# A two-layer hybrid backbone on one core: order of the modulation, of the products in the RWKV doubling and of its scan, layers written out

## What is computed

```
mod = silu(cvec) @ w_ada + b_ada            # shift, scale, gate: 6 x 512 columns, two condition vectors
h = rmsnorm(x) * (1 + scale) + shift
z = h @ w_in                                # 74 tiles of 128 columns
y_a = hyena(z)                              # filters from a small MLP with two sines, long convolution by FFT
y_b = rwkv7(z)                              # two directions, 8 heads of 64
y_c = diff_attention(z)
x = x + gate * ((g_a*(y_a@w0) + g_b*(y_b@w1) + g_c*(y_c@w2)) @ w_out)
```

```
sa = S @ (-kk_t);  S = S * w_t + outer(sa, kk_t * a_t) + outer(v_t, k_t);  y_t = S @ r_t
```

## Time and profile before

| | |
|---|---|
| time, median of 3 runs | 3057.24 us (3052.05 to 3060.49) |
| the profiled execution | 3055.59 us, its span 3053.9 us |
| TensorE busy | 2821.3 us, 92% |
| VectorE, ScalarE, GpSimd busy | 1167.8, 628.5, 161.1 us |
| mean granted clock of TensorE | 0.93 |

### The profile page before, as it was taken

One profiled execution on the slowest core, in us unless ns is written; L12 is line 12 of the kernel. 1 busy time (PEld: TensorE's weight loads), 2 busy tenths in 40 slices (PEclk: granted clock), 3 DMA queues, 4 the chain that ended last, 5 costly groups with the idle time before them and its releaser, 6 DMA issues.

```text
span 3053.9 us, 57422 instructions
## 1 busy us (share of the span) xinstructions
PE 2821.3 (92%) x25584; PEld 1753.7 (57%) x25584; DVE 1167.8 (38%) x1890; ACT 628.5 (21%) x1182; POOL 161.1 (5%) x192
## 2 busy tenths in 40 slices
PE   7999998988898889999999999988889899899998
PEld 2546664575757575555525557545757576655554
DVE  4252725745454631100142536356353636311111
ACT  2111124322232321000031111243232323200000
POOL 0010000010101000000000100000101010000000
PEclk9999999979787989999999999998797888899999
DMA  6211110100000001111161111101000000011111
GB/s 241 95 45 55 49 56 7 43 5 29 5 29 4 30 3 56 62 62 62 56 213 56 45 55 57 41 14 36 4 30 3 30 10 23 14 59 62 62 55 62
DMA packets 38273, 147.13 MB, mean 48 GB/s; under 512 B 4720, under 2 KB 4720, under 8 KB 37136
## 3 DMA queue, kind: packets, MB, share of 16 engines
q1 hardware_dynamic: 34704, 128.47, 12.6%
q0 software_dynamic: 3328, 15.02, 1.3%
HBM read 139.27 MB, written 4.19 MB: 47 GB/s over the span
## 4 chain that ended last, share of the span: by engine, by line
PE 84%; DVE 8%; issue 3%; ACT 3%; DMA 1%; POOL 0%; DVEq 0%; POOLq 0%; another core or an unknown queue 0%; ACTq 0%
PE ps L508 82%; DVE scr L1687 1%; DVE scr L1709 1%; DVE scr L1866 1%; DVE scr L1700 1%; DVE scr L1822 1%; PE ps L873 1%; DVE scr L1859 1%; PE ps L966 1%; DVE scr L1699 0%; ACT scr L1397 0%; PE ps L764 0%; DVE scr L1862 0%; ACT scr L1398 0%; DVE scr L1833 0%
## 5 line engine op out<-in xcount | busy, mean ns | idle before, releaser
L508 PE MATMUL ps<-h,ring 128*128 128x512 f32 (+1 forms) x4480 | 1230.5, 435 | 3.2 <-issue 3.2
L508 PEld LDWEIGHTS ps<-h,ring 128*128 128x128 f32 x4480 | 685.3, 191 | 548.6 <-issue 547.6
L508 PE MATMUL ps<-scr 32*32 32x32 f32 (+9 forms) x17704 | 821.0, 246 | 122.4 <-issue 48.6
L508 PEld LDWEIGHTS ps<-scr 32*32 32x32 f32 (+5 forms) x17704 | 625.4, 140 | 306.1 <-issue 203.0
L1915 DVE SCALAR_TENSOR_TENSOR scr<-scr,ps 128x640 f32<-128x640 f32 x48 | 39.4, 821 | 509.3 <-PE ps L508 508.8
L1455 ACT ACTIVATE scr<-ps 128x640 f32<-128x640 f32 x48 | 33.8, 704 | 561.3 <-PE ps L508 561.3
L508 PE MATMUL ps<-scr,ring 128*128 128x512 f32 (+1 forms) x512 | 139.0, 434 | 4.0 <-DVEq L1920 4.0
L1411 ACT ACTIVATE scr<-ps 128x160 f32<-128x160 f32 x192 | 62.5, 325 | 279.0 <-PE ps L508 278.2
L508 PEld LDWEIGHTS ps<-scr,ring 128*128 128x128 f32 x512 | 77.4, 191 | 65.6 <-issue 65.6
L508 PE MATMUL ps<-scr,cst 128*128 128x512 f32 (+1 forms) x288 | 92.7, 459 | 9.6 <-ACT scr L1375 9.6
L508 PE MATMUL ps<-ring,sc 128*2 128x512 f32 x192 | 88.5, 616 | 8.3 <-ACT lora L1142 8.3
(11 more groups left out here) (254 smaller groups left out, 2189.2 us busy)
## 6 DMA issues: line engine op xcount, KB each, us to landing
ring<-in_w SPq DMA_DIRECT2D x240, 512.0 KB, 3.3
x<-in_x SPq DMA_DIRECT2D x1, 2560.0 KB, 15.8
yc<-in_win POOLq DMA_DIRECT2D x2, 1280.0 KB, 7.8
out_y<-x POOLq DMA_DIRECT2D x1, 2560.0 KB, 7.7
scr<-in_inv POOLq DMA_DIRECT2D x2, 1152.0 KB, 5.3
scr<-in_tab POOLq DMA_DIRECT2D x4, 512.0 KB, 8.9
cst<-in_cst POOLq DMA_DIRECT2D x1, 1466.0 KB, 9.3
scr<-in_ck POOLq DMA_DIRECT2D x2, 256.0 KB, 3.3
```

Source lines behind the costliest of these rows:

```text
L508: return nc.tensor.matmul(out, lhsT, rhs, start=start, stop=stop)
```

## The change

- The modulation leaves the front. A row is now made by four matmuls a slot, each with a stationary side of 128x32 and 256 columns, that write four different quarters of the partitions; small products with a constant matrix `pick` add up the quarters and turn the row. Layer 0's shift and scale come before everything (16 slots, with the squares of x between them), layer 1's between the tiles of layer 0's `w_out`, with the squares of x, and each layer's gate between the gate tiles of attention.
- h is taken tile by tile by the first tile of z. The filter MLP and the filters stand between the first tiles of z, and on VectorE the windows between the taps.
- In the RWKV doubling, A's blocks come ahead of the transposes of K and B. Products go by pairs of chunks into banks 4 and 5 and are read before the next pair: B by ScalarE (1024 columns, 1024, 512), K by VectorE with its mask, within levels 2, 3 and 4. The turned A goes to bank 4 and is copied for itself, the values' products to bank 5.
- In the scan, R comes in by a matmul with the identity in front of `reader`'s product (all four latent chunks), and VectorE's two additions fall away. Transitions and readers are copied together. The values' parts of y move behind the first state step, the state terms of K behind U.
- y is stored in eight pieces by SyncE, each when its tile of x is done.
- The loops over the layers are written out; the last layer makes no modulation. The number of slots stays 240.

```diff
-ORDER = [("filt",)] + [("ada", n, q) for n in range(6) for q in range(4)]
+ADA = [("ada", n, q) for n in range(4) for q in range(4)]
...
-ORDER += [("z", f"av{j}") for j in range(JT)] + [("z", f"ag{j}") for j in range(JT)]
+ORDER += [("z", f"av{j}") for j in range(JT)]
+for _j in range(JT):
+    ORDER += [("z", f"ag{_j}")] + GATE[2 * _j:2 * _j + 2]
...
-ORDER += [("out", j) for j in range(KD)]
+for _j in range(KD):
+    ORDER += [("out", _j)] + ADA[2 * _j:2 * _j + 2]
...
+            for k in range(KD):
+                sp.wait_ge(out_read, k + 1)
+                sp.dma_start(A["y"][:, k * T:(k + 1) * T], xt(k)).then_inc(y_stored, 16)
+            sp.wait_ge(y_stored, 16 * KD)
...
+            def rows_of_mod(bank, q, w):
+                for kk in range(2):
+                    k = 2 * q + kk
+                    for half in range(2):
+                        at = 64 * kk + 32 * half
+                        o = kk * 512 + half * 256
+                        i = mm(ps[at:at + 32, 512 * bank:512 * bank + 256], sc[:, 32 * k:32 * k + 32], w[:, o:o + 256], q == 0, q == 3)
+                i.then_inc(w_used, 1)
+            def turn_row(cols, row):
+                for c in range(4):
+                    half = c // 2
+                    i = mm(cols[:, 2 * c:2 * c + 2], row[:, c % 2 * 128:(c % 2 + 1) * 128], con("pick")[:, 2 * half:2 * half + 2], True, True)
+                return i
...
+            for n in range(4):
+                if n >= 1:
+                    pe.wait_ge(pre_row, n)
+                for q in range(4):
+                    i = 4 * n + q
+                    pe.wait_ge(w_full[i % RING], 16 * (i // RING + 1))
+                    rows_of_mod(0, q, ringslot(i))
+                    if n in (1, 2):
+                        k = 4 * n - 4 + q
+                        pe.wait_ge(pre_sq, k + 1)
+                        sum_of_squares(k).then_inc(pre_sq_used if k < KD - 1 else sums_ready, 1)
+                if n >= 1:
+                    turn_row(mod_bank[:, 8 * (n - 1):8 * n], modrow[(n - 1) % 2]).then_inc(pre_turned, 1)
+            pe.wait_ge(pre_row, 4)
...
+                z_tile("hv0", as_h_comes=True, first_marks=True)
+                z_tile("hx0")
+                pe.wait_ge(hid_ready, 1)
+                wide_mm(6, fw[64:128, 0:64], hid[64:128, :], rows=slice(0, 64)).then_inc(hid_full, 1)
+                z_tile("hv1")
+                pe.wait_ge(hid_ready, 2)
+                filters(0)
+                filters(1)
+                z_tile("hx1")
+                filters(2)
+                filters(3)
+                z_tile("hv2")
+                filters(4)
+                z_tile("hx2")
+                turn_p(0)
+                z_tile("hv3")
+                turn_p(1)
+                z_tile("hx3")
...
+                        def products_of_B(c):
+                            pe.wait_ge(A_read, 4 * g + c // 2)
+                            product(Bt, c, 0)
+                            product(Bt, c + 1, 1).then_inc(A_full, 1)
+                        def products_of_context():
+                            pe.wait_ge(A_read, 4 * g + 2)
+                            product(Bt, 4, 0)
+                            product(Kt, 4, 1).then_inc(A_full, 1)
+                        def products_of_K(c):
+                            pe.wait_ge(A_read, 4 * g + 3)
+                            pe.wait_ge(K_read, 3 * g + 1 + c // 2)
+                            product(Kt, c, 0)
+                            product(Kt, c + 1, 1).then_inc(A_full, 1)
+                        def read_side():
+                            pe.wait_ge(K_read, 3 * g + 3)
+                            for c in range(4):
+                                i = nc.tensor.transpose(ps[:, 2048 + c * 128:2048 + (c + 1) * 128], AR[:, c * 256:c * 256 + 128], ident)
...
+                        products_of_B(0)
                         for lev in range(4):
                             y_of_blocks(lev, 0)
                             y_of_blocks(lev, 1)
-                            if lev < 2:
-                                product(Bt, 2 + 2 * lev)
                             if lev == 3:
-                                product(Kt, 2)
+                                products_of_K(0)
                             blocks_joined(lev, 0)
                             blocks_joined(lev, 1)
                             if lev == 0:
-                                product(Bt, 3)
-                            if lev == 2:
-                                pe.wait_ge(A_read, 4 * g + 2)
-                                product(Kt, 0)
-                                product(Kt, 1)
-                        product(Kt, 3)
-                        product(Kt, 4)
+                                products_of_B(2)
+                            if lev == 1:
+                                products_of_context()
 
                         for hh in range(2):
                             pe.wait_ge(T_ready, 12 * g + 9 + hh)
+                            if hh == 0:
+                                pe.wait_ge(A_read, 4 * g + 3)
                             for c in range(NT):
                                 for e, f in pairs32(d):
                                     i = mm(block_bank(hh)[f, c * 32:(c + 1) * 32], t3(ABQ[hh], 256)[e, c, f], unit(Tc, 32, hh, c)[e], True, True)
                             i.then_inc(Y_full, 1)
+                        products_of_K(2)
                         for hh in range(2):
                             pe.wait_ge(Y_ready, 12 * g + 9 + hh)
...
                         def transition(n, c):
+                            at = transition_in(states_bank(half_of(n)), n)
                             for hh, hr in heads_of_tile:
-                                mm(pt_bank(n)[hr], ident[hr, hr], ident[hr, hr], True, False)
+                                mm(at[hr], ident[hr, hr], ident[hr, hr], True, False)
+                                mm(at[hr], u_part(c, hh, 1), head_cols(Btok, c, hh), False, True)
+                        def reader(n, c):
+                            at = reader_in(states_bank(half_of(n)), n)
                             for hh, hr in heads_of_tile:
-                                i = mm(pt_bank(n)[hr], u_part(c, hh, 1), head_cols(Btok, c, hh), False, True)
-                            return i
...
+                        pe.wait_ge(K_read, 3 * (g + 1))
+                        for c in range(4):
+                            for hh in range(2):
+                                i = mm(ps[:, 2560 + c * 128 + 64 * hh:2560 + c * 128 + 64 * hh + 64], AKQ[hh][:, c * 256:c * 256 + 128], head_cols(vtok, c, hh), True, True)
+                        i.then_inc(X_full, 1)
                         pe.wait_ge(A_read, 4 * (g + 1))
-                        for c in order[1:3]:
-                            i = x_of_values(c)
+                        for hh in range(2):
+                            i = mm(ps[:, 2048 + 64 * hh:2048 + 64 * hh + 64], AKQ[hh][:, 1024:1152], head_cols(vtok, 4, hh), True, True)
                         i.then_inc(X_full, 1)
-                        x_of_values(4).then_inc(X_full, 1)
-                        for c in order[3:5]:
-                            i = x_of_values(c)
-                        i.then_inc(X_full, 1)
+                        pe.wait_ge(TT_ready, 16 * (g + 1))
+                        pe.wait_ge(X_ready, 2 * g + 1)
+                        for half in range(2):
+                            for n, c in enumerate(order[1 + 2 * half:3 + 2 * half]):
+                                for hh in range(2):
+                                    o = 3072 + 512 * half + (c % 2) * 256 + 128 * hh
+                                    i = mm(ps[:, o:o + 128], TT[hh][:, c * 128:(c + 1) * 128], joint_x(c, hh), True, True)
+                            i.then_inc(U2_full, 1)
...
-                                        i = mm(ps[:, o:o + 128], TT[hh][:, cc], joint_x(c, hh), True, True)
-                            i.then_inc(U2_full, 1)
+                        y_of_values(4)
+                        pe.wait_ge(X_ready, 2 * g + 2)
+                        for hh in range(2):
+                            i = mm(ps[:, 2176 + 64 * hh:2176 + 64 * hh + 64], TT[hh][:, 512:640], x_ctx[:, 64 * hh:64 * hh + 64], True, True)
+                        i.then_inc(U2_full, 1)
 
                         pe.wait_ge(U2_ready, g + 1)
+                        pe.wait_ge(masked, 2 * (g + 1))
                         for n in (1, 2):
-                            i = transition(n, order[n])
+                            transition(n, order[n])
+                        for n in (1, 2):
+                            i = reader(n, order[n])
                         i.then_inc(PT_full, 1)
...
+                        transition(3, order[3])
+                        for n in (3, 4):
+                            i = reader(n, order[n])
+                        i.then_inc(PT_full, 1)
```

(103 more changed lines are left out.)

437 lines of the change are left out of this document (217 added, 220 removed).

## The result

The kernel after takes 3208.76 us (median of 4 runs, 3197.42 to 3220.57); before, run beside it, 3058.86 (4 runs, 3052.05 to 3066.05). The ratio is 1.049, 95% interval 1.0438 to 1.0542: slower, where the forecast was 3033 us and faster. The profiled execution took 3197.42 us, its span 3195.6 at a mean granted clock of 0.905 (0.930 before).

A forecast was written before the change was run, and what follows sets the result against it. TensorE's own queue was taken to bound the kernel (84% of the chain). Outside the scan -48 us, scan +1.5 a direction or +24, sum -24: 3033 us, faster; forecast's own range 3008 to 3055, over all 2976 to 3070.

The forecast's parts named there:

- scan proper: Last part of each scan direction: eight added identity matmuls, two heads side by side, cost +0.9 us a direction.
- Fronts and end: Everything outside the scan: layer 0's front -20 us, layer 1's -27, gate rows +8.5, end -9.6; sum -48.
- layer 0's z at 49 us: Layer 0's front: first tile of z starts at 49 us instead of 86, after modulation slots and an uncovered stretch of 9.1.
- rival D: Fronts don't shorten: layer 0 waits on DMA, idle 9 us come twice with low clock; fronts give 20, 3060 us; chance 0.08.
- rival B: Modulation slots: the four column quarters run one after another, +44 us and some +4, 3081 us; chance 0.07.
- Levels: Four doubling levels of each scan direction: fewer product chunks -1.7 us, a new mask wait 0.4; -1.3 a direction.
- Level for 64: Doubling level for 64: last K pairs stand ahead of its joins and wait for a mask; +2.2 us a direction.
- rival C: Doubling levels: the mask before the K pairs becomes the path, +4.5 us a direction, 3081 us; chance 0.11.
- Head: Start of each scan direction, A's blocks to level 0: A's blocks ahead of the transposes, mean -0.2 us a direction.
- rival A: The scan gains: pairs fill gaps between levels, masks leave the path, -24 us in the scan, 2985 us; chance 0.22.

The follow-up runs named there:

- all identities first: Against the kernel after: per bank, all identity matmuls of transitions and readers, then all products, only the first identity starting the accumulation; 3066.64 us, ratio to before 1.0023.
- regrouped kernel: Against the kernel after: in `transition()` and `reader()`, both heads' identities and then both heads' products; 3095.59 us, ratio to before 1.012.
- moving the products: Against the kernel with all identities first: last two chunks' key products issued behind level 4's joins, not ahead of them; 3036.34 us, ratio to before 0.9901.

## Why the prediction was wrong

**The step that failed** is the scan proper: "Eight identity matmuls, 16 records of 128 columns with two heads side by side ... +0.9." They aren't side by side in the code that the diff shows, and the loop over the heads took that from the products beside them too, 56 records a direction in the two functions. Measured +9.5 a direction, 152 us, more than the 142 that the kernel lost in all. The price per record came from a long run of one shape; the order around the new instructions was never walked, though the old `transition()` had two loops where the new one has one. The trace of before had shown that a run of four such records takes 0.26 us to the next shape (in the direction of the earlier trace rows at 691.50, 691.76 and 692.02 us); what a run of two takes was in no row. No rival held it either. With all identities first the term is +1.15, and without the readers' identities 0.90 less than that, so the size was right for an order that wasn't there.

**Fronts and end, right in the sum.** -48 forecast; -50 between the traces, -54 (0.9825) alone. By parts: up to layer 0's first block of A -14.3 us (forecast -15.8 with half the gate rows), from layer 0's scan to layer 1's first block -24.7 (forecast -22.8), behind the last direction -11.2 (forecast -9.6). So no large errors cancel. But the step that gave layer 0's z at 49 us was wrong by 7: its slots waited longer for DMA, as in the first half of the prediction's rival D. The first two tiles then lost 1.9 us (19.4 for 17.5), where 3.8 were set down. In the sum D is refuted, and the prediction's rival B by 0.54 us a slot, under the 0.6 named.
The Trainium skill (TensorE: Matmul & The Clock Gate, "The mechanism" of Part 3) lets a weight load overlap running matmuls only where its row group differs; a sentence ahead of that rule also names the background weight buffer. Taken as the prediction took it, the rule doesn't hold here: the quarters share all rows and still run together, as do two heads with 128 rows each in the regrouped kernel. The measurement decides.

**Levels, right**: -1.0 for -1.3. **Level for 64, right**: +2.5 for +2.2, and moving the products took 1.4 of it back. The prediction's rival C, the masks on the path, asked for +4.5 a direction from these steps together; they gave +1.3, and +2.3 with the head's.

**Head, wrong by 1.2 us a direction** (19 us in all): +1.0, not -0.2. I priced transposes and product pairs at the full clock, 1.1 each. In three backward directions the clock was full, and the stretch took 3.14 us, as forecast (3.2). In the other 13 it was at half for 2.5 us or more of it. The ten transposes took 2.3 to 2.4 us in twelve of these, not 1.3; the product pairs stayed at 1.1 to 1.3 in all but three.

**The prediction's rival A** had the scan faster. Levels alone were (-1.0), but the level for 64 gives that back twice.

What stays open: why the clock fell a second time in seven of 16 directions. The traces show this much. In those seven it had risen late, 4.8 to 5.4 us behind the first matmul of U; in the nine where it stayed up it had risen 2.2 to 4.4 us behind it. In the regrouped kernel six directions rose as late, 4.9 to 5.4 us behind, and none fell. So the second fall came only where a late rise and the per-head order met; what in that order brings it about wasn't isolated.

## What to carry to other kernels

Price a small matmul with its neighbours: walk the issue order of the new code and count the runs of one shape, since a run of two records took as long as one of four. Where heads or tiles lie in two halves of the array, keep one loop for each kind of matmul, not one loop over the heads with both kinds in it. And test parts of a change by themselves: here the fronts gained 1.75%, and one loop header in each of two functions lost 113 us.

## What the runs showed of the hardware

- A run of matmuls of one tile shape had a least time to the next shape. At the full clock it was 0.26 us with 64 columns moved and 0.36 to 0.37 with 128, the same for two records in one column half and four in both, and the same whether or not the next run wrote the same output. At the half clock it was 0.40 and 0.61. In a run of eight at the full clock a 128-column record took 0.066 us (0.53 for the eight).
- Four quarters of columns over the same 128 rows ran together at 0.068 us a record of 256 columns, at full clock.
- In seven of 16 directions TensorE's granted clock rose to 2.4 GHz, and 3.4 us later fell back to 1.2 GHz for 13.65 us, while the engine was busy at every moment by the profile's count, with short runs of alternating shape. In nine directions with the same instructions, and in all of the regrouped ones, it stayed up once it had risen.
